# Seven block products for eight in the last feed-forward layer of a fp32-split decoder step

## The chip, the cores and the metric

The kernel runs on one core of one Trainium2 chip. The metric is the device time of one execution in microseconds (us). TensorE is PE in the profile (PEld its weight loads), VectorE is DVE, ScalarE is ACT, GpSimd is POOL and SyncE is SP.

## The reference, cut to what matters

One inference step of a two-layer decoder, for a prompt of 1024 tokens and 32 sample tokens with the same weights. Each layer has a mixer (gated DeltaNet and gating, or mLSTM), and then this part, which the change touches in layer 1 alone:

```
h = rmsnorm(x, gl[2])
x = x + rmsnorm(jnp.square(jax.nn.relu(h @ w_ff1[l])) @ w_ff2[l], gl[3])
```

`h` has 1024 features, `w_ff1` is 1024x4096 and `w_ff2` is 4096x1024, all in fp32.

## The kernel before

The tokens are in two groups: group 0 has 512, group 1 has 512 and the 32 of the sample, 544 in all. Activations lie with features on the 128 partitions and tokens along the free axis. A fp32 product is made of three products of split operands: each weight and each activation is written as a high part (fp32r) and the rest, and TensorE adds high times high, high times rest, and rest times high in PSUM.

All dense work is a list of 384 **units**. A unit is one 512 KB piece of a weight matrix, 128x1024 in SBUF: for the first feed-forward matrix ("f1") 128 output features over the 8 contraction tiles, for the second ("f2") 256 output features over 4 tiles. The last layer of group 1, `ff(1, 1)`, is 64 units: 8 blocks of four f1 units and four f2 units. SP loads a unit's weights into `wst` (two buffers), ScalarE copies them to the high part `whi` (`hi`, recorded at line 1148), VectorE subtracts and writes the rest `wlo` (`lo`, line 1665), and TensorE takes the unit in four pieces of two contraction tiles (`piece`, line 605 through `mm`). In group 1 the 544 columns go as two matmuls of 272, so a unit has 8 x 3 x 2 = 48 matmuls.

After an f1 unit ScalarE applies relu from PSUM into `relu2`, squares it into `h1hi` and once more in place, and VectorE makes the rest `h1lo` (`h1_rest`, line 1681). After each of the two outputs of an f2 unit VectorE adds PSUM to the accumulator in SBUF (line 1740). In the first f2 unit of a block the contraction tiles are the four f1 units just made, in the order of `steps_of`.

`Plan.order` is one list of items, written out once and walked by every engine in that order. ("d", u, p) is piece p of unit u. Each engine has its own code for an item: ScalarE makes the high part of unit u+1 at ("d", u, 0), VectorE its rest at ("d", u, 1), and both take results at the piece that ends them. So on each engine what stands behind a waiting instruction waits too. `mix` spreads side items (norm, output, mixer work) evenly over the pieces. In `ff(1, 1)` the side items are norm 14 of group 0 (`on`, and eight `ap`, an apply of two VectorE operations each, lines 1777 and 1782) and four `y` (output of group 0: 8 transposes, two copies of PSUM, a store), spread with 14 empty ones over 240 pieces. `link` makes VectorE wait for its own last instruction.

The dense PSUM tile `DB` has four banks. A group 1 output takes a pair of them, so at any time two are in use.

GpSimd does little but issue transfers; its arithmetic in the profile is at lines 2546 (mixer) and 2658 (the last output rows).

## Time and profile before

| | |
|---|---|
| median of 3 runs | 2651.72 us (2650.94 to 2652.86) |
| the profiled execution | 2652.95 us |
| its span in the trace | 2651.1 us |
| PE busy | 2584.7 us, 97% |
| DVE busy | 1381.5 us, 52% |
| ACT busy | 1127.6 us, 43% |
| POOL busy | 243.7 us, 9% |
| mean granted TensorE clock | 0.993 |

The profiled execution took 1.85 us more than its span. Busy time of PE is modelled from pipelined matmuls, and says only that the engine had work. Whether another engine sets the pace is read from the chain that ended last and from the gaps of PE.

### The profile page before, as it was taken

What the parts mean: (1) busy time and instruction counts of PE and PEld (TensorE: products, weight loads), DVE (VectorE), ACT (ScalarE), POOL (GpSimd) and SP (SyncE); (2) the same over time, 40 slices, a digit from 0 to 9 for tenths busy, and PEclk for the clock granted to TensorE, in tenths of its full rate; (3) what the DMA queues carried; (4) which work ended last, traced back from release to release, by engine and by line L of the source; (5) the groups of instructions that cost most, each with busy time, mean ns of one, the idle gap of its engine ahead of it and who ended that gap; (6) DMA issues with size and microseconds to landing.
All of it is one profiled execution on the core that took longest, in us unless ns stands there. A gap on an engine that the chain in (4) does not pass through costs nothing.

```text
span 2651.1 us, 39320 instructions
## 1 busy us (share of the span) xinstructions
PE 2584.7 (97%) x16324; PEld 2308.4 (87%) x16324; DVE 1381.5 (52%) x2201; ACT 1127.6 (43%) x1914; POOL 243.7 (9%) x396
## 2 busy tenths in 40 slices
PE   9998989999999999999999999999999999999998
PEld 7778878788887798899999989998877888999998
DVE  4746764656564465434444465535544456454344
ACT  6654446455444245333333345433332345333324
POOL 4121111100101001100000001110000000000000
PEclk9999999999999999999999999999999999999999
DMA  7453335533333445543333245554434343233322
GB/s 204 157 158 104 105 106 140 154 97 89 106 91 95 119 144 164 173 121 112 104 95 111 83 132 152 162 149 123 120 119 150 97 121 122 85 112 107 96 88 82
DMA packets 368721, 321.47 MB, mean 121 GB/s; under 512 B 11929, under 2 KB 339667, under 8 KB 368544
## 3 DMA queue, kind: packets, MB, share of 16 engines
q1 hardware_dynamic: 336224, 207.91, 27.2%
q0 software_dynamic: 32320, 111.05, 13.8%
q8 instruction: 130, 2.13, 0.3%
q14 instruction: 47, 0.39, 0.0%
HBM read 261.33 MB, written 57.58 MB: 120 GB/s over the span
## 4 chain that ended last, share of the span: by engine, by line
PE 86%; DVE 6%; ACT 5%; DMA 2%; issue 1%; SPq 0%; DVEq 0%; ACTq 0%
PE dense L605 76%; PE mixer L605 8%; ACT arena L1148 1%; DVE wlo L1665 1%; ACT whi L1148 1%; DMA wst<-in_w_in_even_dram 1%; DVE arena L1890 0%; DMA arena<-xrow 0%; ACT relu L1148 0%; DVE hf L1806 0%; DMA xrow<-arena 0%; ACT L1148 0%; ACT L1153 0%; DVE arena L1892 0%; DVE hlo L1802 0%
## 5 line engine op out<-in xcount | busy, mean ns | idle before, releaser
L605 PE MATMUL dense<-hhi,whi 128*128 128x272 f32 (+1 forms) x3072 | 848.2, 330 | 16.8 <-DVE wlo L1665 11.2
L605 PE MATMUL dense<-hhi,wlo 128*128 128x272 f32 (+1 forms) x3072 | 825.3, 323 | 0.0
L605 PE MATMUL dense<-hlo,whi 128*128 128x272 f32 (+1 forms) x3072 | 825.1, 323 | 0.0
L1665 DVE TENSOR_TENSOR wlo<-wst,whi 128x1024 fp32r<-128x1024 f32 x384 | 472.1, 1229 | 235.0 <-ACT whi L1148 234.1
L1148 ACT ACTIVATE whi<-wst 128x1024 fp32r<-128x1024 f32 x384 | 403.9, 1052 | 419.4 <-PE dense L605 407.9
L605 PEld LDWEIGHTS dense<-hhi,whi 128*128 128x128 f32 x3072 | 515.4, 189 | 72.7 <-DVE wlo L1665 16.4
L605 PEld LDWEIGHTS dense<-hhi,wlo 128*128 128x128 f32 x3072 | 514.4, 189 | 41.8
L605 PEld LDWEIGHTS dense<-hlo,whi 128*128 128x128 f32 x3072 | 516.4, 189 | 37.3 <-issue 0.7
L605 PE MATMUL dense<-h1hi,whi 128*128 128x272 f32 (+1 forms) x1536 | 423.0, 330 | 9.4 <-DVE wlo L1665 5.0
L605 PE MATMUL dense<-h1hi,wlo 128*128 128x272 f32 (+1 forms) x1536 | 414.5, 324 | 0.0
L605 PE MATMUL dense<-h1lo,whi 128*128 128x272 f32 (+1 forms) x1536 | 412.7, 323 | 0.0
L605 PEld LDWEIGHTS dense<-h1hi,whi 128*128 128x128 f32 x1536 | 257.1, 189 | 38.3 <-DVE wlo L1665 8.6
L1681 DVE TENSOR_TENSOR h1lo<-relu,h1hi 128x544 fp32r<-128x544 f32 (+1 forms) x128 | 91.6, 716 | 370.9 <-ACT relu L1148 370.8
L605 PEld LDWEIGHTS dense<-h1hi,wlo 128*128 128x128 f32 x1536 | 257.4, 189 | 21.4
L605 PEld LDWEIGHTS dense<-h1lo,whi 128*128 128x128 f32 x1536 | 257.5, 189 | 20.9 <-issue 0.5
L605 PE MATMUL mixer<-arena 128*128 128x128 f32 (+11 forms) x1552 | 231.9, 294 | 20.3 <-DVE arena L1972 18.0
L605 PEld LDWEIGHTS mixer<-arena 128*128 128x128 f32 (+5 forms) x1552 | 194.7, 174 | 59.6 <-issue 21.0
L1148 ACT ACTIVATE relu<-dense 128x512 f32<-128x512 f32 (+2 forms) x132 | 80.5, 610 | 385.7 <-PE dense L605 385.6
L1740 DVE TENSOR_TENSOR accA<-dense,accA 128x512 f32<-128x512 f32 (+1 forms) x168 | 116.2, 698 | 103.4 <-PE dense L605 103.1
L1756 DVE TENSOR_TENSOR ssum<-ssum,sq 128x512 f32<-128x512 f32 (+1 forms) x98 | 69.3, 707 | 126.0 <-ACT sq L1148 126.0
L1148 ACT ACTIVATE ffh<-dense 128x512 f32<-128x512 f32 (+5 forms) x124 | 62.1, 524 | 168.0 <-PE dense L605 155.4
L1148 ACT ACTIVATE arena<-mixer 128x128 f32<-128x128 f32 (+9 forms) x175 | 63.3, 376 | 102.2 <-PE mixer L605 59.4
(352 smaller groups left out, 1814.5 us busy)
## 6 DMA issues: line engine op xcount, KB each, us to landing
wst<-in_w_ff_dram SPq DMA_DIRECT2D x256, 512.0 KB, 3.9
wst<-in_w_in_even_dram SPq DMA_DIRECT2D x48, 512.0 KB, 4.1
wst<-in_w_in_odd_dram SPq DMA_DIRECT2D x48, 512.0 KB, 4.0
proj<-ffh POOLq DMA_DIRECT2D x48, 272.0 KB, 2.6
proj<-ffh POOLq DMA_DIRECT2D x48, 256.0 KB, 2.3
arena<-proj POOLq DMA_DIRECT2D x16, 512.0 KB, 4.8
wst<-in_w_out_even_dram SPq DMA_DIRECT2D x16, 512.0 KB, 4.0
arena<-proj POOLq DMA_DIRECT2D x8, 1024.0 KB, 8.1
```

The source lines that it names most:

```text
L605: return pe.matmul(out, lhsT, rhs, start=start, stop=stop)
L1148: return act.activation(out, in_, func, **how)
L1665: TT(wlo[:, u % 2, :], wst[:, u % 2, :], whi[:, u % 2, :].bitcast(F32), ALU.subtract)\
L1681: TT(h1lo[:, k, 0:n], r, h1hi[:, k, 0:n].bitcast(F32), ALU.subtract)\
L1740: TT(v, out_of(key, g), v, ALU.add).then_inc(S("dve_evac"), 1)
L1756: ins = TT(ssum[:, 0:n], ssum[:, 0:n], sq2[:, c % 2, 0:n], ALU.add)
```

## The change

It touches blocks 3 to 7 of `ff(1, 1)`, 40 of its 64 units. There, two f1 units (256 output features) are computed together as a 2x2 by 2x2 block product: the weights are cut in two halves of output features and two of contraction (512), and x in two halves of contraction and two of tokens (272). Seven products of sums take the place of the eight (Strassen's scheme in Winograd's form). A product, item ("p", u, n), is 4 contraction tiles x 3 x one matmul of 272 columns = 12 matmuls. A pair has 84 matmuls, the two units had 96.

- GpSimd makes the sums of weights in fp32 (`weight_sums`, four operations of 128x512 for a pair), and needs both units' raw weights. The second pair of a block is loaded into another buffer, `raw2`, in space of `accA`.
- ScalarE and VectorE split each of the seven weight operands on its own (128x512), into a ring of five quarters.
- VectorE makes the four sums of x once, in fp32, and splits them (`x_sums`, eight items ("t", i, j) over pieces 44 to 83, that is blocks 1 and 2), in operations of 128x1088. Item ("t", 4, 0) waits for the last f1 unit of block 2 (unit 19 of the layer).
- Products 2, 4, 5 and 6 add to a bank after an earlier value in it has been read. VectorE copies products 0 and 2 and ScalarE product 3 to SBUF; VectorE adds products 1, 4 and 5 to those copies; ScalarE takes product 6. Relu and squares go by half rows of 272.
- Norm 14 and the `y` items are spread over pieces 0 to 43 in place of 0 to 239.
- In the first f2 unit of every block, in all layers, output 1 starts after two steps of output 0, not three.
- Three start-up semaphores become one that counts to 3, with the same places.

The diff, cut to its core:

```diff
+SEVEN = range(3, FG)
+RINGS = ((0, 1, 2, 3, 4, 0, 1), (2, 3, 4, 0, 1, 2, 3))
+SEVEN_READ = ("dve", "dve", "dve", "act", "dve", "dve", "act")
+SEVEN_BANK = "XYXZXZX"
+SEVEN_AFTER = {2: 0, 4: 2, 5: 3, 6: 4}
+XC = GN[1] // 2
+KH = KT // 2
...
-        return [(0, 0), (0, 1), (0, 2), (1, 0), (1, 1), (1, 2), (0, 3), (1, 3)]
+        return [(0, 0), (0, 1), (1, 0), (1, 1), (0, 2), (1, 2), (0, 3), (1, 3)]
...
+            if not self.seven(kind, l, g, f):
+                keys = [((u, 0), (0, 1) if u % 2 == 0 else (2, 3))]
+            elif k % 2 == 0:
+                keys = [((u, n), (RINGS[k // 2][n],)) for n in range(7)]
+                self.sums_at[("p", u - 2, 0) if k else ("d", u - 1, 0)] = u
+                self.pair[u] = len(self.pair)
+            else:
+                continue
+            for key, quarters in keys:
+                r = len(self.ops)
+                self.free.append(max([last[q] + 2 for q in quarters if q in last] + [int(r == 1)]))
+                for q in quarters:
+                    last[q] = r
+                self.op[key] = r
+                self.ops.append(key)
+                self.quarter.append(quarters[0])
...
+        self.ahead = {}
+        for u, (kind, l, g, f, k) in enumerate(self.units):
+            if not self.seven(kind, l, g, f):
+                r = self.op[u, 0]
+                self.ahead["d", u, 0] = [r + 1] if r + 1 < len(self.ops) else []
+                if u + 1 in self.pair:
+                    self.ahead["d", u, 2] = [r + 2]
+            elif u in self.pair:
+                r = self.op[u, 0]
+                for n in range(7):
+                    self.ahead["p", u, n] = [r + n + 3]
+                if k == 0:
+                    self.ahead["p", u, 0] = [r + 2, r + 3]
+                else:
+                    self.ahead["p", u, 4], self.ahead["p", u, 5], self.ahead["p", u, 6] = [], [r + 7], []
...
-        self.mix(rows[:-16], rest(2) + self.norm(14, False) + [("y", t) for t in range(4)] + rest(12))
+        n = 2 * PIECES[1] * FK * SEVEN[0]
+        self.mix(rows[:n - 52], rest(2) + self.norm(14, False) + [("y", t) for t in range(4)])
+        sums = [("t", 0, 0)] + [("t", i, j) for i in range(1, 5) for j in range(i == 1, 2)]
+        self.mix(rows[n - 52:n - 12], sums + [("rest",)])
+        self.mix(rows[n - 12:-16], [])
...
-                if u >= 2:
-                    sp.wait_ge(S("w_split"), u - 1)
+                before = PLAN.before_raw[u]
+                if before is not None:
+                    sp.wait_ge(S("w_split"), PLAN.last_op(before) + 1)
+                elif u >= 2:
+                    sp.wait_ge(S("t_split"), 4)
+                if u >= 2 and before != u - 2:
+                    sp.wait_ge(S("w_hi"), PLAN.first_op(u - 2) + 1)
...
+            def seventh(u, n):
+                r = PLAN.op[u, n]
+                pe.wait_ge(S("w_split"), r + 1)
+                if PLAN.pair[u] == 0 and n in (2, 3, 4, 6):
+                    pe.wait_ge(S("t_split"), {2: 2, 3: 1, 4: 4, 6: 3}[n])
+                fresh = n not in SEVEN_AFTER
+                if fresh:
+                    begin((u, n))
+                else:
+                    evac_wait(pe, (u, SEVEN_AFTER[n]))
+                out = DB[:, PLAN.jobs[u, n]["bank"], 0:XC]
+                wh, wl = split_part(whi, hhi[0], PLAN.quarter[r]), split_part(wlo, hlo[0], PLAN.quarter[r])
+                xh, xlow = x_part(hhi, n), x_part(hlo, n)
+                for t in range(KH):
+                    for i, (w, x) in enumerate(((wh, xh), (wh, xlow), (wl, xh))):
+                        last = pe.matmul(out, w[:, t * P:(t + 1) * P], x[:, t, :], start=fresh and t == 0 and i == 0,
+                                         stop=t == KH - 1 and i == 2, skip_group_check=True)
+                        if t == 0 and i == 0:
+                            last.then_inc(S("w_used"), 1)
+                last.then_inc(S("job_done"), 1)
...
+                if n in (0, 1, 6):
+                    v = u + n // 6
+                    act.wait_ge(S(f"w_loaded{v % 2}"), 16 * (v // 2 + 1))
+                else:
+                    act.wait_ge(S("w_sum"), 3 * PLAN.pair[u] + {2: 1, 4: 1, 3: 2, 5: 3}[n])
+                A_(split_part(whi, hhi[0], PLAN.quarter[r]), raw_part(u, n), ACT.Copy).then_inc(S("w_hi"), 1)
...
+                if n == 3:
+                    if PLAN.pair[u]:
+                        evac_wait(act, (min(v for v in PLAN.pair if PLAN.pair[v] == PLAN.pair[u] - 1), 4))
+                    A_(keep[:, 1, :], out, ACT.Copy).then_inc(S("act_evac"), 1)
+                elif n == 6:
+                    r = relu2[:, (f + 1) % 2]
+                    act.wait_ge(S("h1_split"), f)
+                    A_(r[:, 0:XC], out, ACT.Relu).then_inc(S("act_evac"), 1)
+                    evac_wait(act, (u, 6))
+                    squares(u + 1, 0, XC).then_inc(S("h1_hi"), 1)
...
+            def summed(u, n):
+                v, c0 = u + (n == 4), XC * (n > 1)
+                r = relu2[:, PLAN.ff1_rank[v] % 2, c0:c0 + XC]
+                evac_wait(act, (u, n))
+                after(own(A_(r, r, ACT.Relu)))
+                last = squares(v, c0, c0 + XC)
+                if n == 5:
+                    last.then_inc(S("h1_hi"), 1)
...
+                    if item[2] in (3, 6):
+                        seventh(*item[1:])
+                    elif item[2] == 2:
+                        summed(item[1], 1)
+                    elif item[2] == 5:
+                        summed(item[1], 4)
...
+                if i == 0:
+                    dve.wait_ge(S("y_turned"), 9)
+                    done((max(u for u, x in enumerate(PLAN.units) if x[:3] == ("f1", 1, 0)), 0))
+                    link(TT(tsum, h12, h11, ALU.subtract))
+                    link(TT(tsum, tsum, l12, ALU.add))
+                    link(TT(tsum, tsum, l11, ALU.subtract))
+                    return
+                if part == 1:
+                    n = {1: 3, 2: 2, 3: 6, 4: 4}[i]
+                    link(dve.tensor_copy(t_part(hhi, n), tsum))
+                    TT(t_part(hlo, n), tsum, t_part(hhi, n).bitcast(F32), ALU.subtract).then_inc(S("t_split"), 1)
+                    return
+                dve.wait_ge(S("t_split"), i - 1)
+                if i == 2:
+                    link(TT(tsum, h22, tsum, ALU.subtract))
+                    link(TT(tsum, tsum, l22, ALU.add))
+                elif i == 3:
+                    link(TT(tsum, h21, tsum, ALU.subtract))
+                    link(TT(tsum, tsum, l21, ALU.add))
+                elif i == 4:
+                    done((min(PLAN.pair) - FK - 1, 0))
+                    link(TT(tsum, h22, h12, ALU.subtract))
+                    link(TT(tsum, tsum, l22, ALU.add))
+                    link(TT(tsum, tsum, l12, ALU.subtract))
...
+                if PLAN.units[u][4] and n == 3:
+                    h1_rest(u - 1)
+                if SEVEN_READ[n] != "dve":
+                    return
+                out = DB[:, PLAN.jobs[u, n]["bank"], 0:XC]
+                if n in (1, 4, 5):
+                    evac_wait(dve, (u, {1: 0, 4: 3, 5: 2}[n]))
+                if n in (1, 4):
+                    dve.wait_ge(S("h1_split"), f - 1 + n // 4)
+                done((u, n))
+                if n in (0, 2):
+                    dve.tensor_copy(keep[:, n, :], out).then_inc(S("dve_evac"), 1)
+                    if PLAN.units[u][4] and n == 0:
+                        h1_rest(u - 2)
+                    return
+                r = relu2[:, (f + (n == 4)) % 2, XC * (n > 1):XC * (n > 1) + XC]
+                TT(r, out, keep[:, {1: 0, 4: 1, 5: 2}[n], :], ALU.add).then_inc(S("dve_evac"), 1)
...
+                    if item[2] in (0, 2):
+                        seventh(*item[1:])
+                    for r in PLAN.ahead[item]:
+                        lo(r)
+                    if item[2] not in (0, 2):
...
+            def weight_sums(u):
+                p = PLAN.pair[u]
+                for v in (u, u + 1):
+                    pool.wait_ge(S(f"w_loaded{v % 2}"), 16 * (v // 2 + 1))
+                if p:
+                    pool.wait_ge(S("w_split"), PLAN.op[next(v for v in PLAN.pair if PLAN.pair[v] == p - 1), 4] + 1)
+                halves = lambda v: (raw(v)[:, 0:KH * P], raw(v)[:, KH * P:2 * KH * P])
+                (a11, a12), (a21, a22) = halves(u), halves(u + 1)
+                add = pool.tensor_tensor
+                step(add(sums[:, 0, :], a11, a21, ALU.subtract))
+                add(sums[:, 1, :], a22, sums[:, 0, :], ALU.subtract).then_inc(S("w_sum"), 1)
+                add(a21, a21, a22, ALU.add).then_inc(S("w_sum"), 1)
+                pool.wait_ge(S("w_split"), PLAN.op[u, 1] + 1)
+                pool.wait_ge(S("w_sum"), 3 * p + 1)
+                add(a12, a12, sums[:, 1, :], ALU.subtract).then_inc(S("w_sum"), 1)
```

## Rows read from the trace of the kernel before

**Rows 1.** Section 4 of the page: the chain that ended last, by line.

```profile
PE dense L605 76%; PE mixer L605 8%; ACT arena L1148 1%; DVE wlo L1665 1%; ACT whi L1148 1%; DMA wst<-in_w_in_even_dram 1%; DVE arena L1890 0%; DMA arena<-xrow 0%; ACT relu L1148 0%; DVE hf L1806 0%; DMA xrow<-arena 0%; ACT L1148 0%; ACT L1
```

**Rows 2.** The chain in order of time, third block: start us, us, what.

```profile
2324.43 0.74 DVE arena L1740
...
2325.30 47.49 PE dense L605 x378
...
2372.82 0.74 DVE arena L1740
```

**Rows 3.** Timeline, all engines, around a unit's start: start us, us, engine, what.

```profile
2442.38 0.41 PE L605 MATMUL dense<-hhi,whi 128*128 128x272 f32 x2
...
2442.57 0.72 DVE L1740 TENSOR_TENSOR arena<-dense,arena 128x544 f32<-128x544 f32 x1 [2.05 <-PE dense L605]
...
2442.70 1.06 ACT L1148 ACTIVATE whi<-wst 128x1024 fp32r<-128x1024 f32 x1 [4.04 <-PE dense L605]
```

**Rows 4.** Timeline of DVE, block 1: an independent, then a dependent operation.

```profile
2315.25 0.73 DVE L1681 TENSOR_TENSOR h1lo<-relu,h1hi 128x544 fp32r<-128x544 f32 x1 [3.83 <-ACT relu L1148]
2315.89 0.75 DVE L1777 SCALAR_TENSOR_TENSOR hf<-accA,par,rstd 128x512 f32<-128x512 f32 x1
2316.75 0.69 DVE L1782 TENSOR_TENSOR accA<-hf,xl 128x512 f32<-128x512 f32 x1
```

**Rows 5.** ACT groups by shape, whole span: count | busy us, mean ns | idle before.

```profile
L1148 ACT ACTIVATE h1hi<-relu 128x512 fp32r<-128x512 f32 x64 | 40.4, 632 | 2.0
...
L1148 ACT ACTIVATE ffh<-dense 128x272 f32<-128x272 f32 x12 | 4.7, 391 | 0.0
```

**Rows 6.** DVE groups by shape, whole span.

```profile
L1665 DVE TENSOR_TENSOR wlo<-wst,whi 128x1024 fp32r<-128x1024 f32 x384 | 472.1, 1229 | 235.0 <-ACT whi L1148 234.1
...
L1681 DVE TENSOR_TENSOR h1lo<-relu,h1hi 128x512 fp32r<-128x512 f32 x64 | 45.2, 706 | 146.0 <-ACT relu L1148 145.9
...
L1995 DVE TENSOR_TENSOR arena<-arena,mixer 128x256 f32<-128x256 f32 x32 | 13.1, 420 | 13.0 <-PE mixer L605 12.7
```

**Rows 7.** Section 6 of the page: a weight load, from issue to landing.

```profile
wst<-in_w_ff_dram SPq DMA_DIRECT2D x256, 512.0 KB, 3.9
```

**Rows 8.** Timeline, DVE and POOL, at three of the POOL operations.

```profile
337.21 2.68 DVE L1665 TENSOR_TENSOR wlo<-wst,whi 128x1024 fp32r<-128x1024 f32 x1 [2.03 <-ACT whi L1148]
337.49 1.30 POOL L2546 TENSOR_TENSOR arena<-arena 128x512 f32<-128x512 f32 x1
...
666.67 1.30 POOL L2546 TENSOR_TENSOR arena<-arena 128x512 f32<-128x512 f32 x1
666.89 1.65 DVE L1681 TENSOR_TENSOR h1lo<-relu,h1hi 128x512 fp32r<-128x512 f32 x1 [1.73 <-ACT relu L1148]
...
747.30 1.31 POOL L2546 TENSOR_TENSOR arena<-arena 128x512 f32<-128x512 f32 x1
747.35 0.69 DVE L1740 TENSOR_TENSOR accA<-dense,accA 128x512 f32<-128x512 f32 x1
```

**Rows 9.** Timeline of PE: the first matmul after an idle time, which stands in brackets.

```profile
171.72 0.50 PE L605 MATMUL dense<-hhi,whi 128*128 128x512 f32 x1 [1.86 <-DVE wlo L1665]
...
358.28 0.58 PE L605 MATMUL mixer<-arena 128*128 128x128 f32 x1 [6.11 <-DVE arena L1972]
...
482.90 0.51 PE L605 MATMUL dense<-hhi,whi 128*128 128x512 f32 x1 [3.10 <-DVE hlo L1802]
...
2217.30 0.50 PE L605 MATMUL dense<-h1hi,whi 128*128 128x512 f32 x1 [2.12 <-DVE wlo L1665]
```

**Rows 10.** Stretches from those matmuls on: us, then PE, PEld, DVE, ACT, POOL busy, PEclk.

```profile
171.72:176.00 4.28, 4.28 (x18) 3.29 (x18) 1.22 (x1) 1.06 (x1) 1.49 (x2) 1.00 0.80 208
...
358.28:362.00 3.72, 3.72 (x19) 3.72 (x20) 3.69 (x7) 0.00 (x0) 0.00 (x0) 0.60 0.23 55
482.90:492.00 9.10, 7.93 (x20) 4.63 (x21) 8.49 (x12) 3.15 (x5) 0.00 (x0) 0.62 0.20 59
2217.30:2223.00 5.70, 5.70 (x18) 4.54 (x19) 4.68 (x7) 3.90 (x6) 0.00 (x0) 0.70 0.32 92
```

More of the change, by code:

```diff
@@ L95, in unit, with seven, parts, first_op @@
         return rows
+    @staticmethod
+    def seven(kind, l, g, f):
+        return kind == "f1" and (l, g) == (1, 1) and f in SEVEN
+    def parts(self):
+        last, prior = {}, {}
+        self.op, self.ops, self.quarter, self.free = {}, [], [], []
+        self.before_raw, self.sums_at, self.pair = {}, {}, {}
+        for u, (kind, l, g, f, k) in enumerate(self.units):
+            place = (u % 2, k // 2 if self.seven(kind, l, g, f) else 0)
+            self.before_raw[u] = prior.get(place)
+            prior[place] = u
+            if not self.seven(kind, l, g, f):
[15 more added lines that the diff above has]
+        self.ahead = {}
+        for u, (kind, l, g, f, k) in enumerate(self.units):
+            if not self.seven(kind, l, g, f):
[11 more added lines that the diff above has]
+                    self.ahead["p", u, 4], self.ahead["p", u, 5], self.ahead["p", u, 6] = [], [r + 7], []
+    def first_op(self, u):
+        return self.op[u, 0] if (u, 0) in self.op else self.op[u - 1, 2]
+    def last_op(self, u):
+        return (self.op[u, 5] if u in self.pair else self.op[u, 0]) if (u, 0) in self.op else self.op[u - 1, 6]
     def linear(self, kind, l, g, seq=None, gate=None):
@@ L112, in ff @@
             for k in range(FK):
-                rows += self.unit("f1", l, g, f, k)
+                if not self.seven("f1", l, g, f):
+                    rows += self.unit("f1", l, g, f, k)
+                elif k % 2 == 0:
+                    u = len(self.units)
+                    self.units += [("f1", l, g, f, k), ("f1", l, g, f, k + 1)]
+                    rows += [[("p", u, n)] for n in range(7)]
             for k in range(FK):
@@ L292, in count @@
                 wide = g
+            elif item[0] == "p":
+                u, n = item[1:]
+                key, bank = (u, n), SEVEN_BANK[n]
+                begun_at = {"X": 0, "Y": 1, "Z": 3}[bank]
+                if n == begun_at:
+                    b = min(range(4), key=ended_at)
+                    self.jobs[key] = dict(bank=b, before={last[b]} if b in last else set())
+                    last[b] = (u, {"X": 6, "Y": 1, "Z": 5}[bank])
+                    self.jobs.setdefault(last[b], dict(bank=b))
+                rank += 1
+                reader = SEVEN_READ[n] + "_evac"
+                evac[reader] += 1
+                self.jobs.setdefault(key, {}).update(bank=self.jobs[u, begun_at]["bank"], done=rank,
+                                                     read=(reader, evac[reader]))
+                continue
             elif item[0] in ("on", "gate", "gate2", "misc"):
@@ L328 @@
 PLAN = Plan()
+PLAN.parts()
 def build(nc, x_prompt, x_sample, state_gdn, state_gdn_conv, state_mlstm_c, state_mlstm_n, state_mlstm_m,
@@ L1719, in unit_begin @@
             def unit_begin(u):
                 kind, l, g, a, k = PLAN.units[u]
+                if kind == "f2" and k == 0 and PLAN.seven("f1", l, g, a):
+                    h1_rest(u - 2)
                 if kind == "f1" and k or kind == "f2" and k == 0:
@@ L2663, in _ @@
             for item in PLAN.order:
+                if item in PLAN.sums_at:
+                    weight_sums(PLAN.sums_at[item])
                 if item[0] == "d":
```

105 lines of the change are left out of this document (80 added, 25 removed).

## Prediction

> **What bounds the kernel now.** I read the page first, for the chain that ended last: 76% of it is TensorE's dense work at one line, and no other entry but the mixer's matmuls has more than 1% [rows 1]. So removed matmuls are worth their full time only while VectorE and ScalarE deliver operands and empty banks on time. Then I took the chain in order of time in the layer that is changed: 47.5 us without a break, and one VectorE addition of 0.74 us at the end of each block's first f2 unit, where both bank pairs come free at once [rows 2]. A block of 8 units takes 2372.82 - 2324.43 = 48.39 us. Less about 0.3 us for that addition, a unit takes 6.01 us, and a matmul of 272 columns 6.01 / 48 = 0.1253 us. The timeline around a unit's start gives the hand-over times that a schedule needs: with the new unit's first matmul at 2442.38, VectorE starts on the unit just ended 0.19 us later, and ScalarE on what needs that first matmul 0.32 us later [rows 3]. On VectorE an independent operation starts 0.07 to 0.1 us before its forerunner's recorded end, one that waits for its forerunner 0.10 us after it [rows 4]. From a released operand to TensorE it is 0.14 us (the chain's part between addition and matmul: 2325.30 - 2324.43 - 0.74, [rows 2]).
>
> **The change part by part.**
>
> *Matmuls removed.* 10 pairs by 12 matmuls by 0.1253 us = **-15.0 us**, at the same clock. A product's 12 matmuls take 1.50 us, a pair 10.5 us instead of 12.0.
>
> *The sums of x.* 18 VectorE operations of 128x1088 between pieces 44 and 83. From 1229 ns for 1024 elements and 706 for 512 [rows 6], 1.02 ns per element, one costs about 1.29 us, and 1.39 with the wait for itself. What matters is what stands behind them on VectorE. Item ("t", 0, 0) falls just after the first piece of block 1's first f2 unit. There VectorE makes h1's last rest from 2.3 to 3.0 us after the unit's start, then the three sums to 7.1, the next unit's rest to 8.4, and only then reads the unit's first output, to 9.0. The next unit could start at 6.3 and starts at 9.1: **+2.8 us**. The next five items fall where VectorE has time: a unit of 6.0 us holds 2 to 2.7 us of its other work, and the item 2.6. Item ("t", 4, 0) stands after the last piece of unit 18 and waits for unit 19's end. Behind it stand `h1_rest(18)` and `lo(20)`, and TensorE needs the latter right after unit 19. The path is 0.19 + 3 x 1.39 + 0.66 + 1.23 + 0.14 = **+6.4 us**, with nothing over it: TensorE has no other work in the list there. The last item, ("t", 4, 1), lies beside unit 20. If a 1088 operation takes 1.2 or 1.4 us, both terms move by 3 x 0.1, some 0.6 us together.
>
> *Norm 14 and the outputs, closer together.* One more VectorE pair of 1.44 us [rows 4] delays a bank in block 0: **+0.35 us**. The rest has room, since an `ap` comes every three or four pieces, 4.5 us or more.
>
> *ScalarE in a pair.* Seven high parts of 512 at 0.53 us each (632 ns less the overlap of 0.1, [rows 5]), one copy and one relu of 272 from PSUM at 391 ns [rows 5], and eleven operations of 272 in SBUF. That shape is not in the trace: from 1.06 us for 1024 [rows 3] and 0.632 for 512 [rows 5], 0.83 ns per element, it costs 0.43, and 0.46 in a chain. In all 9.1 us of 10.5. It fits, but without play: relu and squares of products 1, 4 and 5 follow each other, and product 6's relu comes after them. In each block's first f2 unit output 1 needs product 6's bank 1.5 us after the unit's start and gets it 0.34 us late: 5 x 0.34 = **+1.7 us**. With 0.04 us more for each ScalarE operation, put through the same schedule, another 3.9 us come on top; that is the upper bound of the term. The boundary stall of 0.3 us that every block has comes once more, because block 3 was spared before: **+0.3 us**.
>
> *VectorE in a pair, alone.* Seven rests of 512 at 0.62 us, two of 544 at 0.66, five reads of PSUM at 0.37 (420 ns for 256 columns, [rows 6], less the overlap): 7.5 us of 10.5. Alone it is in time everywhere, by 0.1 to 0.5 us.
>
> *GpSimd's sums and VectorE.* Four additions of 128x512 a pair, 1.30 us each [rows 8]. Two rows decide this term. At 666.89 a `h1lo` of VectorE starts while such an addition runs, takes 1.65 us and not 0.7, and ends 0.57 us after GpSimd's end. At 337.21 a `wlo` that began 0.28 us before GpSimd's takes 2.68 us, and ends 1.10 us after it. GpSimd's own time stays 1.30. The addition at 747.35, which has one operand in PSUM, takes its usual 0.69 us beside GpSimd [rows 8]. So a VectorE operation with two operands in SBUF stands still for as long as GpSimd's runs, and reads of PSUM don't. All rests are of the first kind.
>
> The schedule of the first pair of a block, in us from product 0's start. ScalarE ends product 2's high part at 0.32 + 0.63 = 0.95. That releases the load of the next pair's second unit, which lands 3.9 later [rows 7], at 4.9. GpSimd starts its sums at 5.05. VectorE's queue is then: rest of product 5, rest of 6, rest of the next pair's 0, and behind these the addition for product 4, for which product 6 waits. The rests end at 6.9, 8.8 and 10.6, each behind one GpSimd addition of 1.3 us. The addition for product 4 ends at 11.0, and product 6 starts at 11.1, not 9.0: **5 x 2.1 = +10.6 us**. The second pair has no such burst, since the next sums wait for loads that follow f2's last units. In the f2 units a burst meets a VectorE that is half idle, and moves nothing on the path. Bounds: nothing if the three rests slip past the burst; 5 x 3.0 if the load lands 0.6 us later and pairs drag each other. I take the rows' 2.1, which hardly depends on who goes first when both ask.
>
> The Trainium skill (SBUF — State Buffer, section "SBUF: two separate sides") states this as a lock: a VectorE operation with two SBUF inputs and a GpSimd operation that reads SBUF exclude each other for the whole instruction, and the first to start keeps it. The trace agrees on the exclusion (1.65 and 2.68 us), but the operation that started 0.28 us earlier did not keep it. By this rule and by the rows the sum is the same to 0.1 us; if no such rule held, it would be 10.6 us and its clock share less.
>
> *TensorE's clock after new stalls.* After an idle time of 1.86 us the clock stays at 1.00; after 2.12, 3.10 and 6.11 us it is at half for a while, 1.2 and not 2.4 GHz [rows 9, 10]. What that took is length by (1 - PEclk): 5.70 x 0.30 = 1.7 us, 9.10 x 0.38 = 3.5, 3.72 x 0.40 = 1.5. The stall of 6.4 us is like the last: **+2.0**, with 3.5 as its upper bound. That of 2.8 lies between the first two: **+1.7** (0 to 3.5). The five of about 2.0 us lie between the idle time that cost nothing and the one that cost 1.7; I take 0.4 each, **+2.0** (0 to 8.5).
>
> *Costed at nothing.* The new order in the first f2 unit: output 1 starts 0.75 us earlier in group 1, at 1.50 us, and its bank is read by ScalarE 0.19 + 0.62 us after the start and free at 0.95. In group 0 four single banks leave more room. If that cover went, it would cost up to 0.75 us in 27 places. The start-up semaphore counts in the same places. The loads are as many as before, and land 2 us or more before they are read.
>
> **The sum.** -15.0 + 2.8 + 6.4 + 0.35 + 1.7 + 0.3 + 10.6 = +7.1, and +5.7 for the clock: **+12.8 us**. Against the profiled execution, 2652.95 (span 2651.1 and 1.85 around it), that is 2665.7; it stands 1.2 above the median, so the forecast for the median is 2651.7 + 12.8 = **2664.5 us**. A changed block should take 48.4 - 3.0 + 2.1 + 0.34 = 47.8 us at full clock, hardly less than before: the gain of the matmuls is given back where it arises, and the sums of x come on top.
>
> **The rivals.**
>
> *GpSimd's bursts miss the path (the other side).* Place: the first pair of each block, product 6's wait. If the next pair's load lands late enough (after 7 us), or VectorE gets its rests done between two of GpSimd's additions, the 10.6 and their 2.0 of clock are gone: 2651.7 + 0.2 = 2651.9 us. For it: VectorE's need in that stretch is only three rests of 0.6 us, and the GpSimd addition at 747.30 met none of them at all [rows 8]. Against it: loads land in 3.9 us evenly, three additions come in a row, and the queue is in order. It decides from a loss under 1 us a block on; then the change is within 0.2%.
>
> *ScalarE becomes the bound.* With 0.06 us more per operation its 20 operations a pair need 10.3 of 10.5 us, and products 3, 4 and 6 are handed over late in both pairs: +6 us more, 2670 to 2672 us. For it: the half rows cost almost what full ones do. Against: the shapes are bounded closely by rows.
>
> *The waits of the x sums are hidden and so is the burst.* That would need VectorE to reach `lo(20)` before unit 19 ends; what the lines say speaks against it. It gives 2651.9 - 8.4 = 2643.5 us.
>
> **How the numbers follow.** Forecast with its own spread (2658 to 2670) 0.60; bursts miss the path 0.19; ScalarE bound or still more clock loss (2670 to 2676) 0.14; hidden sums 0.07. A difference under 0.2% (5.3 us) is about what a measurement of this kernel can't tell from none. The range runs from 2650 to 2672 us: it takes in most of the first rival and half of the second. Slower by over 0.2%: 0.58 of the forecast's 0.60, and the 0.14, with a little of the second case, 0.74. Within: 0.19. Faster: 0.07.
>
> **What the profile after would show.** Right: in the chain, a VectorE stretch of some 6 us before block 2's first f2 unit and one of 3 us in block 1's; in each changed block a PE gap of about 2 us before product 6 of the first pair, with VectorE's rests at 1.3 to 2 us and not 0.69; PEclk under 1.00 after the long gap. Wrong: no gap before product 6, rests that stay at 0.69 beside GpSimd, or a gap that ScalarE ends. The prediction fails most likely in the burst term, whose place hangs on 1 or 2 us of a load's landing.

## The result: slower by 0.15%, and the profile after

The changed kernel takes 2656.47 us (median of 22 runs, 2653.62 to 2661.18), the one before 2652.88 us (22 runs in turn with it, 2649.75 to 2655.03). The ratio is 1.0015, with a 95% interval of 1.0009 to 1.0021, so the change costs 3.6 us. The interval leaves out 1, so the sign is sure, but the size lies under the 0.2% that I had set as the bound of "no change". I had forecast 12.8 us.

The page after, first line and the chain that ended last by line, to be held against [rows 1]:

```profile
span 2655.5 us, 39542 instructions
...
PE dense L735 71%; PE mixer L735 8%; PE dense L805 3%; DVE wlo L1867 2%; ACT arena L1302 1%; ACT whi L1302 1%; DMA wst<-in_w_ff_dram 1%; ACT relu L1302 1%; DVE wlo L1871 1%; DVE arena L2151 0%; DMA arena<-xrow 0%; ACT h1hi L1302 0%; DVE hf L2067 0%; DMA wst<-in_w_in_even_dram 0%; ACT L1302 0%
```

The seven products are the new entry `PE dense L805`. VectorE's rests now stand in the chain with 2% and 1% (`wlo`, L1867 for whole units, L1871 for quarters). Where in the layer that is, the chain in order of time shows. The columns are start us, us, what; [rows 2] are its counterpart.

```profile
2326.55 1.30 DVE accA L1935
...
2327.88 1.31 DVE accA L1936
2329.20 1.30 DVE accA L1937
2330.53 1.23 DVE wlo L1867
2331.75 0.64 DVE arena L2001
...
2332.53 42.46 PE dense L735 x336
...
2375.43 1.30 DVE accA L1953
2376.76 1.30 DVE accA L1954
2378.08 1.30 DVE accA L1955
2379.41 0.72 DVE h1lo L1887
2380.13 1.15 DVE wlo L1867
...
2381.32 7.39 PE dense L735 x42
...
2416.92 0.44 DVE relu L1976
...
2417.50 12.56 PE dense L805 x96
```

Three places are to be seen. At 2326.55 the first item of x sums, with the next unit's rest and a read of PSUM behind it. At 2375.43 the item that waits for unit 19, with two rests behind it. At 2416.92 product 4's addition, for which product 6 waits. PE's timeline gives the idle time ahead of each, in brackets:

```profile
2332.53 0.49 PE L735 MATMUL dense<-h1hi,whi 128*128 128x272 f32 x2 [2.73 <-DVE arena L2001]
...
2381.32 0.82 PE L735 MATMUL dense<-h1hi,whi 128*128 128x272 f32 x2 [6.35 <-DVE wlo L1867]
...
2417.50 0.37 PE L805 MATMUL dense<-hhi,whi 128*128 128x272 f32 x1 [0.47 <-DVE relu L1976]
```

2.73 us where I said 2.8, and 6.35 where I said 6.4; but 0.47 before product 6, which with its slower first matmuls makes product 6 0.7 us late, where I said 2.1. The windows of these places, with the same columns as [rows 10], show what the clock did: from the matmul after the 2.73 us on, from the one after the 6.35 us on, and over one whole changed block.

```profile
2332.53:2336.00 3.47, 3.47 (x27) 3.47 (x28) 3.44 (x4) 1.06 (x1) 0.00 (x0) 1.00 0.47 151
2381.32:2388.00 6.68, 6.68 (x38) 6.68 (x39) 3.65 (x4) 1.06 (x1) 0.00 (x0) 0.69 0.47 158
...
2429.89:2476.67 46.78, 46.11 (x363) 45.38 (x361) 30.43 (x40) 22.41 (x45) 11.82 (x8) 1.00 0.30 90
```

PEclk is 0.69 after the long gap, which costs 6.68 x 0.31 = 2.1 us. After the gap of 2.73 us and in the blocks it is 1.00. A changed block takes 46.78 us; one of before 48.39 [rows 2].

For the experiments a finer measure than the total is wanted, since the clock grants in earlier stages differ from run to run. I use the stretch from the first matmul of block 0's first f2 unit to that of block 7's, read from PE's timeline ("layer" below): before 343.05 us, after 345.62. Behind it both take 38.5 us, and ahead of it the profiled run of after is 1.8 us later. About 0.9 of these are work that has moved: the two matmuls of norm 14's sum stand inside the stretch in the kernel before, and ahead of it (2271.35) in after and in every changed kernel. The first line is of before, the second of after:

```profile
2286.50 1.02 PE L605 MATMUL dense<-ssum,ones 128*128 128x512 f32 x2
```

```profile
2259.97 1.02 PE L735 MATMUL dense<-ssum,ones 128*128 128x512 f32 x2
```

From the matmul before them to the second behind them it is 1.36 us (2286.25 to 2287.61), where the same dense matmuls alone take 0.50. So 0.86 us have to be added to the 2.57 of the stretch, and the layer costs 3.4 us, close to the total's 3.6. Ahead of it about 0.9 us are left. One stretch of lower clock from 1743.8 us on, where before has none, costs more than that (2.2 us at 0.50 and 3 us at 0.80, 1.7 us). The stretch starts between 2268.0 and 2272.6 us in the changed kernels, so nothing can be read from such a difference, and the new order in the first f2 units of the earlier layers shows no price in it.

### The profile page after: what moved, and what is told of

Same layout as the page of the kernel before. It is cut to its first block, busy times and chain, and to the rows that moved or that the text cites. A ratio compares the mean times of both kernels' runs of the same rounds, so it can differ in the third digit from the quotient of the medians.

```text
span 2655.5 us, 39542 instructions
## 1 busy us (share of the span) xinstructions
PE 2580.0 (97%) x16204; PEld 2299.7 (87%) x16204; DVE 1460.7 (55%) x2319; ACT 1160.7 (44%) x2034; POOL 302.8 (11%) x436
## 4 chain that ended last, share of the span: by engine, by line
PE 84%; DVE 7%; ACT 5%; DMA 2%; issue 2%; SPq 0%; DVEq 0%; ACTq 0%
PE dense L735 71%; PE mixer L735 8%; PE dense L805 3%; DVE wlo L1867 2%; ACT arena L1302 1%; ACT whi L1302 1%; DMA wst<-in_w_ff_dram 1%; ACT relu L1302 1%; DVE wlo L1871 1%; DVE arena L2151 0%; DMA arena<-xrow 0%; ACT h1hi L1302 0%; DVE hf L2067 0%; DMA wst<-in_w_in_even_dram 0%; ACT L1302 0%
## 5 line engine op out<-in xcount | busy, mean ns | idle before, releaser
L735 PE MATMUL dense<-hhi,whi 128*128 128x272 f32 (+1 forms) x2752 | 782.7, 335 | 16.7 <-DVE wlo L1867 11.5
L735 PE MATMUL dense<-hhi,wlo 128*128 128x272 f32 (+1 forms) x2752 | 759.9, 327 | 0.0
L735 PE MATMUL dense<-hlo,whi 128*128 128x272 f32 (+1 forms) x2752 | 759.4, 327 | 0.0
L1302 ACT ACTIVATE whi<-wst 128x1024 fp32r<-128x1024 f32 (+1 forms) x389 | 397.9, 1024 | 417.9 <-PE dense L735 404.3
L1867 DVE TENSOR_TENSOR wlo<-wst,whi 128x1024 fp32r<-128x1024 f32 x364 | 447.1, 1228 | 225.6 <-ACT whi L1302 224.5
L735 PEld LDWEIGHTS dense<-hhi,whi 128*128 128x128 f32 x2752 | 466.2, 189 | 73.0 <-DVE wlo L1867 16.8
L735 PEld LDWEIGHTS dense<-hhi,wlo 128*128 128x128 f32 x2752 | 464.9, 189 | 42.1
L735 PEld LDWEIGHTS dense<-hlo,whi 128*128 128x128 f32 x2752 | 466.7, 189 | 37.5 <-issue 0.7
L1302 ACT ACTIVATE relu<-dense 128x512 f32<-128x512 f32 (+3 forms) x122 | 71.9, 589 | 318.4 <-PE dense L735 318.4
L1302 ACT ACTIVATE relu<-relu 128x272 f32<-128x272 f32 (+2 forms) x178 | 99.6, 560 | 29.6 <-DVE relu L1976 24.7
```

The costliest lines, as they stand in the source:

```text
L735: return pe.matmul(out, lhsT, rhs, start=start, stop=stop)
L1302: return act.activation(out, in_, func, **how)
L1867: TT(wlo[:, u % 2, :], wst[:, u % 2, :], whi[:, u % 2, :].bitcast(F32), ALU.subtract)\
```

## What ended product 6's wait

This is VectorE and GpSimd around the first pair of block 3, whose product 0 starts at 2407.84. The timeline of after answers to [rows 8]. L1871 are VectorE's rests, L2926 to L2928 GpSimd's additions:

```profile
2412.90 1.85 POOL L2926 TENSOR_TENSOR accA<-accA 128x512 f32<-128x512 f32 x1 [4.12 <-DMA accA<-in_w_ff_dram]
2412.91 0.68 DVE L1871 TENSOR_TENSOR wlo<-wst,whi 128x512 fp32r<-128x512 f32 x1
2414.07 1.23 DVE L1871 TENSOR_TENSOR wlo<-wst,whi 128x512 fp32r<-128x512 f32 x1 [0.48 <-ACT whi L1302]
2414.83 1.62 POOL L2927 TENSOR_TENSOR accA<-accA 128x512 f32<-128x512 f32 x1
2415.23 1.77 DVE L1871 TENSOR_TENSOR wlo<-accA,whi 128x512 fp32r<-128x512 f32 x1
2416.41 1.73 POOL L2928 TENSOR_TENSOR accA<-accA 128x512 f32<-128x512 f32 x1
2416.92 0.43 DVE L1976 TENSOR_TENSOR relu<-dense,accA 128x272 f32<-128x272 f32 x1
```

The burst is where I placed it: GpSimd starts 5.06 us after product 0, the addition for product 4 stands behind the rests, and the read of PSUM at 2416.92 isn't held though GpSimd runs (0.43 us). But the first rest takes 0.68 us. It is recorded 0.01 us after GpSimd's operation, and still it is GpSimd's record that is longer, 1.85 us for 1.30. Then the second rest takes 1.23, GpSimd's next 1.62, the third rest 1.77.

The ends (start and duration added) tell more than the durations. Rest, addition, rest, addition, rest, addition end at 2413.59, 2414.75, 2415.30, 2416.45, 2417.00 and 2418.14. A rest ends 0.55 us after the addition before it, and an addition 1.14 to 1.16 us after the rest before it; in the other four changed blocks it is 0.54 to 0.56 and 1.13 to 1.17. This fits one operation at a time, in turns, with the wait inside the record of the one that waits. That neither is slowed otherwise is read from these ends and not tested by a run of its own. The held `h1lo` of [rows 8] shows the same distance: it ends 0.57 us after GpSimd's end.

So the rests end 5.75, 7.46 and 9.16 us after product 0, where I had 6.9, 8.8 and 10.6. Of the last difference, 1.15 us come from the first rest, which stood behind no addition. The other 0.3 come from the turn of addition and rest, which takes 1.70 us and not 1.3 + 0.57. The addition for product 4 starts 9.1 us after product 0 and not 10.6.

Who came first was a near tie. In the other four blocks the first rest is recorded 0.09 to 0.22 us before GpSimd's first addition, and is served first as well.

## The experiments

Each was timed in five rounds against the kernel before. The layer column is the stretch defined above, of the one profiled run of each; before has 343.05 there, or 342.2 without the sum of norm 14 that the others have ahead of it.

| kernel | median, us | ratio to before [95%] | layer, us | PE's idle times over 0.4 us, behind the first, of 0.52, that all show in block 0 (e7 in block 1) |
|---|---|---|---|---|
| after | 2656.47 | 1.0015 [1.0009, 1.0021] | 345.62 | 2.73, 6.35, 5 x 0.47 |
| e1 wait item behind unit 20 | 2651.82 | 0.9995 [0.9986, 1.0004] | 342.38 | 2.73, 3.09, 5 x 0.46 |
| e2 GpSimd adds nothing | 2651.33 | 0.9995 [0.9986, 1.0004] | 340.66 | 2.73, 6.35 |
| e3 product 4 read first | 2656.21 | 1.0012 [1.0004, 1.0021] | 345.43 | 2.75, 6.35, 5 x 0.62 |
| e4 products 4, 5 read first | 2650.77 | 0.9994 [0.9985, 1.0003] | 341.06 | 2.75, 6.35 |
| e5 e1, and first item earlier | 2649.81 | 0.9990 [0.9980, 0.9999] | 338.48 | 3.09, 5 x 0.46 |
| e6 e5 and e4 | 2644.69 | 0.9972 [0.9961, 0.9982] | 333.71 | 3.04 |
| e7 four blocks changed | 2658.62 | 1.0024 [1.0015, 1.0032] | 349.23 | 2.75, 6.00, 4 x 0.46 |
| e8 first GpSimd sum twice | 2656.44 | 1.0014 [1.0005, 1.0023] | 345.28 | 2.73, 6.35, 5 x 0.46 |
| e9 e6, wait item behind unit 21 | 2639.31 | 0.9956 [0.9943, 0.9970] | 330.05 | none |
| e10 e4, half-row relu twice | 2656.64 | 1.0019 [1.0010, 1.0028] | 345.71 | 2.73, 6.35, 5 x 0.52 to 0.61 |

**GpSimd's part: e2.** GpSimd's four additions of weights are left out and only their semaphore counts stay, so products 2 to 5 work on other weights, and the outputs have other values.

```diff
-                step(add(sums[:, 0, :], a11, a21, ALU.subtract))
-                add(sums[:, 1, :], a22, sums[:, 0, :], ALU.subtract).then_inc(S("w_sum"), 1)
-                add(a21, a21, a22, ALU.add).then_inc(S("w_sum"), 1)
+                pool.sem_inc(S("w_sum"), 1)
+                pool.sem_inc(S("w_sum"), 1)
...
-                add(a12, a12, sums[:, 1, :], ALU.subtract).then_inc(S("w_sum"), 1)
+                pool.sem_inc(S("w_sum"), 1)
```

> The changed kernel in which GpSimd does none of its four additions a pair, only the waits and the semaphore counts, so the products use what lies in the operands' places. Theory (GpSimd's additions hold up VectorE's rests, and with them product 6 of each first pair by 0.7 us): the rests take 0.69 us all over, the gap before product 6 goes, a changed block takes 46.0 us in place of 46.76, 3.5 to 4.5 us less in all, ratio 1.0000. Rival (ScalarE's 20 operations a pair set the pace of the first pair, and VectorE waits for them): the blocks stay within 0.2 us of 46.76, ratio 1.0015.

The groups of VectorE's quarter rests in the changed blocks (count, busy us, mean ns), first of after, then of e2:

```profile
L1871 DVE TENSOR_TENSOR wlo<-accA,whi 128x512 fp32r<-128x512 f32 x35 | 32.7, 946 | 5.3 <-ACT whi L1302 5.0
L1871 DVE TENSOR_TENSOR wlo<-wst,whi 128x512 fp32r<-128x512 f32 x25 | 29.8, 1190 | 2.7 <-ACT whi L1302 2.4
```

```profile
L1871 DVE TENSOR_TENSOR wlo<-accA,whi 128x512 fp32r<-128x512 f32 x35 | 23.6, 687 | 5.3 <-ACT whi L1302 5.0
L1871 DVE TENSOR_TENSOR wlo<-wst,whi 128x512 fp32r<-128x512 f32 x25 | 17.2, 687 | 2.7 <-ACT whi L1302 2.4
```

Without GpSimd every rest takes 687 ns. The 60 rests lose 62.5 - 40.8 = 21.7 us to it, yet a block falls only from 46.8 to 45.8 us and the layer by 4.96. So GpSimd's additions cost the path 1.0 us a block, not the 2.1 (and clock) that I had given them, and VectorE's spare time swallows the rest. The two long gaps stay as they were. The theory is borne out, by slightly more than it said (3.5 to 4.5 us), and the rival, ScalarE as the pace, is not.

**Which wait carries it: e3 and e4.** In the first pair of a block VectorE reads a finished product before it makes the rest ahead, for product 4 (e3), or 4 and 5 (e4, whose lines are these).

```diff
-                    if item[2] in (0, 2):
+                    early = (0, 2, 4, 5) if PLAN.units[item[1]][4] == 0 else (0, 2)
+                    if item[2] in early:
                         seventh(*item[1:])
                     for r in PLAN.ahead[item]:
                         lo(r)
-                    if item[2] not in (0, 2):
+                    if item[2] not in early:
```

> The changed kernel, in which VectorE in the first pair of a block reads product 4 before it makes the rest that stands ahead of it. Theory A (product 6 waits only for this addition's place in VectorE's queue, and VectorE has the time): the gap before product 6 goes, 3.5 us less, ratio 1.0002. Theory B (VectorE is short of time while GpSimd's additions run, and the delay moves to the next hand-over, the read of product 0 of the second pair): the gap before product 6 goes and one of about the same size comes at product 2 of the second pair, ratio 1.0012 to 1.0018.

> As the one before, but products 4 and 5 both are read before the rests that stand ahead of them, in first pairs. Theory A (queue order alone): 3.5 us less, ratio 1.0002, no gap over 0.15 us within pairs. Theory B (VectorE short of time): some of it comes back at the second pair, total gain between 1.5 and 3 us, ratio 1.0004 to 1.0010.

In e3 the gap before product 6 is gone, and one of 0.62 us stands in the second pair, at product 2. VectorE's timeline of e3 in block 3, and PE's row:

```profile
2414.75 0.44 DVE L1976 TENSOR_TENSOR relu<-dense,accA 128x272 f32<-128x272 f32 x1 [0.37 <-PE dense L805]
2415.11 2.67 DVE L1871 TENSOR_TENSOR wlo<-accA,whi 128x512 fp32r<-128x512 f32 x2
2417.70 0.43 DVE L1976 TENSOR_TENSOR relu<-dense,accA 128x272 f32<-128x272 f32 x1
2420.08 0.69 DVE L1871 TENSOR_TENSOR hlo<-accA,hhi 128x512 fp32r<-128x512 f32 x1 [1.95 <-ACT hhi L1302]
2420.69 0.43 DVE L1971 COPY accA<-dense 128x272 f32<-128x272 f32 x1
```

```profile
2421.26 0.36 PE L805 MATMUL dense<-hhi 128*128 128x272 f32 x1 [0.62 <-DVE accA L1971]
```

Product 4 is now read at 2414.75, at once. Product 5 still waits for two rests that GpSimd stretches, to 2417.70. The copy at 2420.69, for which the second pair's product 2 waits, stands behind a rest that waits until 2420.08 for ScalarE, which has product 5's relu and squares ahead of that high part. One queue position moved the stall and saved nothing (1.0012), as theory B had it. With both reads first (e4) no gap over 0.4 us is left in the changed blocks, a block takes 45.8 to 46.0 us, and the layer falls by 4.6 us, nearly as far as without GpSimd's additions and further than either theory said (3.5 us). GpSimd does the same work in e4 as in after: what it costs depends on which operations stand behind the held ones.

**Is the loss GpSimd's time: e8.** The first of its additions is done twice, the same sum into the same place.

```diff
                 step(add(sums[:, 0, :], a11, a21, ALU.subtract))
+                step(add(sums[:, 0, :], a11, a21, ALU.subtract))
```

> The changed kernel in which GpSimd makes the first of its four additions twice, 1.3 us more in a burst. Theory (the additions and VectorE's rests exclude each other and take turns, so each more that VectorE meets costs it up to 1.3 us, of which product 6 feels 0.5 to 1.3): 2.5 to 6.5 us slower than the changed kernel, ratio 1.0024 to 1.0040, and the gap before product 6 grows to 1.2 us or more. Rival (GpSimd is hidden): ratio 1.0015.

The ratio is 1.0014, that of after: my theory's value missed, the rival's was met. GpSimd's and VectorE's timelines of e8 around the burst:

```profile
2409.73 1.68 POOL L2926 TENSOR_TENSOR accA<-accA 128x512 f32<-128x512 f32 x1 [3.22 <-DMA accA<-in_w_ff_dram]
...
2414.76 1.73 POOL L2929 TENSOR_TENSOR accA<-accA 128x512 f32<-128x512 f32 x1
```

```profile
2409.57 0.68 DVE L1871 TENSOR_TENSOR wlo<-wst,whi 128x512 fp32r<-128x512 f32 x1
2410.72 1.23 DVE L1871 TENSOR_TENSOR wlo<-wst,whi 128x512 fp32r<-128x512 f32 x1 [0.47 <-ACT whi L1302]
2411.88 1.78 DVE L1871 TENSOR_TENSOR wlo<-accA,whi 128x512 fp32r<-128x512 f32 x1
2413.58 0.43 DVE L1976 TENSOR_TENSOR relu<-dense,accA 128x272 f32<-128x272 f32 x1
```

The rests take 0.68, 1.23 and 1.78 us, as in after. The additional operation lengthens the burst behind product 4's read, where nothing on the path waits. So the price in this place goes by the rests and additions that come between the burst's start and the critical read, not by GpSimd's busy time.

**The x sums' places: e1, e5, e6, e9.** The item that waits for unit 19 goes behind unit 20 (e1), the first item also up to before block 1's first f2 unit (e5), both with e4's order (e6), and at last the waiting item behind unit 21 (e9). The lines of e9; e1 has the lines of ('t', 4, 0) and ('t', 4, 1) alone, with 20 and 21, and e5 has all three items, with 20, 21 and 11. e6 and e9 also have e4's lines:

```diff
+        u0 = len(self.units) - 64
+        self.order.remove(('t', 4, 0))
+        self.order.insert(self.order.index(("d", u0 + 21, 1)) + 1, ('t', 4, 0))
+        self.order.remove(('t', 4, 1))
+        self.order.insert(self.order.index(("d", u0 + 22, 1)) + 1, ('t', 4, 1))
+        self.order.remove(('t', 0, 0))
+        self.order.insert(self.order.index(("d", u0 + 11, 1)) + 1, ('t', 0, 0))
```

> The changed kernel with items (t,4,0) and (t,4,1) moved behind VectorE's rest for the unit after next: (t,4,0) to after piece 1 of unit 20, (t,4,1) to after piece 1 of unit 21. Theory (the gap of 6.35 us before unit 20 is nothing but VectorE's queue standing in this item's wait, and the half clock after it is its consequence): the gap goes, PEclk stays 1.00 there, 6.5 + 2.1 = 8.6 us less than the changed kernel, so 5.0 us under the kernel before, ratio 0.998. Rival (the sums' own VectorE time is what is missing, and the wait only says where): the gap comes back within the next two units as 3 us or more, ratio 0.9995 or above.

> The changed kernel with (t,4,0) and (t,4,1) behind unit 20 and 21 as in e1_wait_later, and (t,0,0) moved ahead, to after piece 1 of unit 11. Theory (each of the two stalls comes from the one item's place in VectorE's queue, and VectorE has room beside f1 units): both gaps go, 8.6 and 2.5 us less in the layer than in the changed kernel. Rival (the three operations of 1.3 us delay the next rest wherever they stand): the second gap is only moved.

> Both moves of e5_both_moves, and VectorE reads products 4 and 5 of first pairs before the rests, as in e4_reads_first_4_5. If the three losses are independent: what e5_both_moves gains plus what e4_reads_first_4_5 gained over the changed kernel. If they aren't, less than that by over 2 us.

> As e6_moves_and_reads, but (t,4,0) stands after piece 1 of unit 21 and (t,4,1) after piece 1 of unit 22. In e6_moves_and_reads a gap of 3.04 us stood before unit 21, with VectorE's three sums in front of the read of unit 20's outputs, both of which end in its last piece. Theory (the sums have room only where the next read of PSUM is not of both bank pairs): that gap goes, and 1.7 us of half clock behind it, 3 to 4.7 us less in the layer, ratio 0.9953 to 0.9961. Rival (VectorE is short of 4 us anywhere in block 2): a gap of 2 us or more before unit 22 or 23.

In e1 the 6.35 us become 3.09, not nothing. VectorE's timeline there:

```profile
2378.45 1.29 DVE L1958 TENSOR_TENSOR accA<-hhi 128x1088 f32<-128x1088 f32 x1
...
2381.10 1.29 DVE L1960 TENSOR_TENSOR accA<-accA,hlo 128x1088 f32<-128x1088 f32 x1
2382.42 1.36 DVE L2006 TENSOR_TENSOR arena<-dense,arena 128x544 f32<-128x544 f32 x2
```

The item no longer waits, but it stands before the reads of unit 20's outputs. Unit 20 is a first f2 unit, whose two outputs both end in its last piece, at 2380.2. VectorE is in its sums until 2382.4, so both bank pairs stay full 2.2 us longer. That is e1's rival, the gap that comes back as 3 us, and its ratio (0.9995) is met too. In e5 the gap of 2.73 us goes and this one stays, so of its theory half holds. In e6 the layer falls by 11.9 us against after, where e5 (7.1) and e4 (4.6) add up to 11.7: the losses are independent. In e9 the item is behind the second piece of unit 21, whose outputs end half a unit apart, and the gap goes, with 3.7 us of the layer, as the theory said. The chain of e9 in order of time, through blocks 1 and 2:

```profile
2319.95 10.54 PE dense L742 x84
...
2331.38 47.49 PE dense L742 x378
...
2378.89 0.73 DVE arena L2008
...
2379.76 18.16 PE dense L742 x144
2397.92 18.24 PE dense L812 x145
```

It is as dense as [rows 2]: the eighteen VectorE operations of the x sums (fourteen of 1.3 us, and four casts of 0.7) lie in these blocks and none is in the chain. e9 takes 2639.31 us against 2650.86 in its rounds, 0.44% less than before, and is the fastest kernel here. Its layer stretch is 13.0 us under that of before, or 12.1 without the sum of norm 14, and the total's difference is 11.6.

**Fewer blocks: e7.** Blocks 4 to 7 are changed, block 3 is not.

```diff
-SEVEN = range(3, FG)
+SEVEN = range(4, FG)
```

> The changed kernel with seven products in blocks 4 to 7 only, the sums of x one block later. Theory (a changed block is worth 48.39 - 46.76 = 1.6 us, and the sums of x cost the same 11 us wherever they stand): 1.6 us slower than the changed kernel, ratio 1.0021. Rival (norm 14 and the outputs, spread over 76 pieces and not 44, give something back): 0.3 to 0.5 us less than that, ratio 1.0019 to 1.0020.

The ratio is 1.0024 for 1.0015. The two intervals overlap, so the totals alone don't settle it, but the layer is 3.6 us longer than in after: each changed block earns something, even in the form of after, and the x sums cost about the same however many blocks use them. Of these 3.6 us, 1.6 are the block's gain. 1.7 are the clock's: after the same gap at the same place, now 2.75 us, PEclk is down, as it is in e1. The windows from the matmul behind the gap on, of e7, then of e1:

```profile
2378.39:2384.00 5.61, 5.61 (x33) 5.61 (x34) 4.28 (x5) 1.06 (x1) 0.00 (x0) 0.70 0.39 116
```

```profile
2330.47:2336.00 5.53, 5.53 (x32) 5.53 (x33) 4.27 (x5) 1.06 (x1) 0.00 (x0) 0.69 0.38 114
```

5.61 x 0.30 = 1.7 us, where after loses nothing.

**ScalarE's room: e10.** To e4, the relu of a half row in SBUF is done a second time, which changes no value and costs ScalarE three operations of 0.43 us more in a pair.

```diff
                 after(own(A_(r, r, ACT.Relu)))
+                after(own(A_(r, r, ACT.Relu)))
```

> As e4_reads_first_4_5, but ScalarE does the relu in place on each of the three half rows of a pair twice, with the same result, some 1.4 us more in a pair. Theory (ScalarE has 9.1 us of work in 10.5 and is not the bound of the changed kernel, but close to it): 23 of 24 parts of that time are now used, and the block grows from 46.0 by 0.5 to 2 us. Rival (ScalarE is the bound already): it grows by the full 2 x 1.4 us.

A block of e4, then one of e10:

```profile
2427.89:2473.70 45.81, 45.50 (x363) 45.12 (x362) 28.98 (x40) 22.27 (x44) 12.31 (x8) 1.00 0.32 93
```

```profile
2427.72:2474.73 47.01, 46.03 (x362) 45.33 (x361) 29.30 (x40) 24.65 (x51) 11.78 (x8) 1.00 0.30 90
```

ScalarE's 24.65 - 22.27 = 2.4 us a block make this block 47.01 - 45.81 = 1.2 us longer, and the layer 4.65 us, 0.9 a block. Four to five tenths come through. A ScalarE that bounds the pairs would hand on all of it, one with room none. So it is close to its limit, but not the bound. Its work in a pair of after is about (22.41 - 4 x 1.06) / 2 = 9.1 us of 10.5, what I had forecast, and the rival of the prediction by which it is the bound (2670 to 2672 us) is refuted by the result and by the gap before product 6, which VectorE ends.

## Why the prediction was right in sign and wrong in size

| term of the prediction | said, us | measured, us | where |
|---|---|---|---|
| matmuls removed | -15.0 | -15.0 | 120 fewer on the page (16204 for 16324), in e9 18.24 us for 145 of them, 0.1258 each |
| item ("t", 0, 0) and ("t", 4, 0) | +2.8, +6.4 | +9.3 together | block 1's first f2 unit to block 2's: 57.71 us of after for 48.40 |
| norm and outputs denser | +0.35 | +0.3 or less | gap of 0.52 us in block 0, where before has 0.22 |
| output 1 waits for product 6's bank | +1.7 | 5 x 0.29 = 1.5 | PE's timeline, first f2 units |
| one more boundary stall | +0.3 | +0.3 or a little more | gaps of 0.16 us, matmul to matmul 0.3 to 0.4 |
| GpSimd's burst | +10.6 | 5 x 1.0 = 5.0 by e2; of it 5 x 0.7 = 3.5 at product 6 | e2, e4 |
| clock after 6.4 us | +2.0 | +2.1 | PEclk 0.69 over 6.68 us |
| clock after 2.8 us | +1.7 | 0 (1.7 in e1, e7) | PEclk 1.00 |
| clock after the five | +2.0 | 0 | PEclk 1.00 in the blocks |

The measured terms add up to 3.5 us. The total says 3.6, and the layer 2.57 + 0.86 = 3.4 with the sum of norm 14 on both sides, so nothing of size is left over.

The mechanism was right at each place: the same three waits, in the same items, with the same releasers. The waits of the x sums were right to 0.1 us together, with some luck: before unit 20 the hand-over took 0.44 us (2374.99 to 2375.43) and not 0.19, and the three sums 3 x 1.32 and not 3 x 1.39. What failed is the size of one term, and the clock with it. 10.6 + 2.0 + 1.7 us were said for the burst and two of the clock terms, and 5.0 were measured; the difference of 9.3 us is the whole of 12.8 - 3.6.

The step that failed is in the schedule of the first pair: "The rests end at 6.9, 8.8 and 10.6, each behind one GpSimd addition of 1.3 us", and with it that the 2.1 us "hardly depends on who goes first when both ask". After shows ends at 5.75, 7.46 and 9.16. Two rests stand behind an addition and not three, since the first rest was served before GpSimd's first addition (1.15 us), and each turn is 1.70 us long and not 1.87 (0.3 us). That a rest stands still beside a GpSimd addition holds: each held rest ends 0.55 us after the addition's end. I had worked the schedule out from single additions in the mixer with one rest beside each [rows 8], which show no second turn. Who goes first is worth 1.15 of the 1.44 us by which the addition for product 4 came earlier.

I had named the condition as a rival's ("gets its rests done between two of GpSimd's additions", 0.19) and its bound, a loss under 1 us a block: the 0.7 us at product 6 lie just inside. The result lies between my two cases, nearer to the rival's: its +0.2 us, with GpSimd's 5.0 and without the 1.7 of clock, is 3.5 us. Some of this is chance. The starts that decided who went first lie 0.01 to 0.22 us apart, and the clock's 1.7 us after the 2.73 us of idle time, absent in after's profiled run, were lost in those of e1 and e7.

The Trainium skill (SBUF — State Buffer, section "SBUF: two separate sides") describes an exclusive lock between a VectorE operation with two SBUF inputs and a GpSimd operation that reads SBUF, which the first to start keeps for the whole instruction. The ends above agree with the exclusion, and the longer records of GpSimd (1.85, 1.62 and 1.73 us for 1.30) hold its wait for the rest ahead of it. The addition with one operand in PSUM, which isn't of that kind, isn't held (0.43 us at 2416.92). Who keeps it can't be told from the recorded starts: the rest recorded 0.01 us later went first here, and at 337.21 VectorE's was recorded 0.28 us earlier and GpSimd's went first [rows 8].

The rival with hidden sums took off only 8.4 us, the long wait with its clock (6.4 + 2.0). With the other wait and its clock (2.8 + 1.7) it would have been 2639.0 us, and e9, in which all three stalls are gone, takes 2639.31.

The changed block was said to take 47.8 us and takes 46.8. So each earns 1.6 us, 8.2 in five, and the x sums' two waits with their clock cost 9.3 + 2.1 = 11.4. So this is where the gain of 15 us went: 6.8 stay in the changed blocks as small stalls (5.0 by GpSimd, the rest in the banks' hand-over), and the x sums take more than what is left. e9 removes the two waits and GpSimd's part without touching the mathematics, by moving items and reads in VectorE's order.

Open is why the clock falls in some kernels after the 2.73 us and not in others, and what decides who goes first when the two engines ask within 0.3 us of each other.

## What to carry to other kernels

An item that is cheap in busy time (4 us of VectorE here) costs what stands behind it in its queue: look for the next operation that TensorE waits for, and put the item behind the reads that free banks, at a unit whose outputs don't end together. Where two engines hold each other up, count the held operations that stand before the critical read and change their order; the helper engine's busy time says little. Lay the ends of both engines' operations side by side: the durations hold the waits, the ends show the turns. Test such an order one read further than seems needed, since a stall that is moved by one position can come back in the next stage.

## What the runs showed of the hardware that I had not expected

- GpSimd additions of 128x512 with both operands in SBUF and VectorE subtractions with two operands in SBUF alternate when both queues are full. GpSimd's records go from 1.30 to between 1.61 and 1.85 us, VectorE's from 0.69 to 1.23 and 1.77, but the ends follow each other by 0.54 to 0.56 us (VectorE behind GpSimd) and 1.13 to 1.17 us (GpSimd behind VectorE), a turn of 1.70 us. An addition done twice (e8) changed the total by nothing that can be measured.
- After the same idle time of TensorE at the same place, 2.73 to 2.75 us, in one profiled run of each kernel, the granted clock was down in e1 and e7 (0.69 and 0.70 over the next 5.5 us, 1.7 us lost) and at 1.00 in after, e2, e3, e4, e8 and e10. After 3.04 to 3.09 us it was down in each of e1, e5 and e6, after 6.00 and 6.35 us in each kernel that had such a gap. In the range of 2.7 us the loss can't be put into a sum as one value.
- A VectorE operation of 128x1088 with a wait for its forerunner has a pitch of 1.32 us, 1.30 of them its own time. The wait costs 0.02 us there, and not the 0.10 that I had taken from operations of 512 elements [rows 4].
